# A mixture-of-experts kernel: gate and up units of whole rows, runs of 8192 bytes, activation work in the down stage

## What is computed

```python
D_MODEL, SEQ, N_EXPERTS, TOP_K, D_EXPERT = 1024, 512, 32, 4, 1024

def clamped_swiglu_expert(xb, w_gu, b_gu, w_dn, b_dn):
    gu = xb @ w_gu + b_gu
    x_glu, x_lin = gu[..., :D_EXPERT], gu[..., D_EXPERT:]
    x_glu = jnp.minimum(x_glu, SWIGLU_LIMIT)
    x_lin = jnp.clip(x_lin, -SWIGLU_LIMIT, SWIGLU_LIMIT)
    act = x_glu * jax.nn.sigmoid(SWIGLU_ALPHA * x_glu) * (x_lin + 1.0)
    return act @ w_dn + b_dn
```

## Time and profile before

| | us |
|---|---|
| median of 3 runs | 1479.59 (1477.33 to 1483.07) |
| profiled execution | 1484.01 |
| its span | 1482.2 |
| first matmul of the loop's first round | 347.02 |
| first down matmul of the last expert | 1452.19 |

### The profile page before, as it was taken

How to read it: one execution, slowest core, us unless ns; L and a number is a source line. 1 busy time by engine, 2 the same in 40 slices (tenths; PEclk the granted TensorE clock), 3 DMA queues, 4 the chain that set the end, 5 groups by cost and what they waited for, 6 DMA issues and landing times.

```text
span 1482.2 us, 19488 instructions
## 1 busy us (share of the span) xinstructions
PE 1397.9 (94%) x6520; PEld 1151.0 (78%) x6520; DVE 1233.7 (83%) x927; ACT 1025.6 (69%) x750; POOL 451.3 (30%) x231
## 2 busy tenths in 40 slices
PE   6999998967999999999999999999999999999995
PEld 5877886855888888788778877877888888788774
DVE  5534545367999999999999999999999999999997
ACT  5234332365888887877778778878877887877774
POOL 0000000275233533333333334433333333333301
PEclk9999998978999999999999999999999999999998
DMA  8311324366999999999999999999999999999994
GB/s 304 102 58 57 100 71 132 117 203 230 369 388 385 387 374 369 369 371 371 362 365 367 359 357 375 366 362 370 365 365 379 372 368 372 371 369 363 369 358 147
DMA packets 129145, 453.48 MB, mean 306 GB/s; under 512 B 13887, under 2 KB 13903, under 8 KB 128992
## 3 DMA queue, kind: packets, MB, share of 16 engines
q1 hardware_dynamic: 117096, 432.55, 78.4%
q0 software_dynamic: 10304, 18.26, 4.8%
q10 hardware_dynamic: 1720, 2.34, 0.5%
HBM read 447.63 MB, written 22.59 MB: 317 GB/s over the span
## 4 chain that ended last, share of the span: by engine, by line
PE 70%; DMA 12%; DVE 6%; issue 6%; ACT 4%; POOL 2%; SPq 0%; ACTq 0%; DVEq 0%; POOLq 0%
PE ps L1670 17%; PE ps L1678 16%; PE ps L1672 16%; DMA raw<-in_w_down 4%; PE ps L1401 4%; PE ps L1402 4%; PE ps L1407 4%; DVE wlo L974 4%; DMA raw_b<-in_w_gate_up 4%; ACT whi L682 3%; DMA raw<-in_w_gate_up 2%; PE ps L1648 1%; PE ps L1661 1%; POOL slot_table L600 1%; DMA xg<-h_rows,idx_gather 1%
## 5 line engine op out<-in xcount | busy, mean ns | idle before, releaser
L974 DVE TENSOR_TENSOR wlo<-raw,whi 128x2048 fp32r<-128x2048 f32 x274 | 646.0, 2394 | 126.3 <-ACT whi L682 125.4
L682 ACT ACTIVATE whi<-raw 128x2048 fp32r<-128x2048 f32 x274 | 521.9, 1915 | 207.3 <-DMA raw<-in_w_down 97.0
L1670 PE MATMUL ps<-whi,xT_hi 128*128 128x512 f32 x1040 | 412.7, 397 | 36.0 <-issue 22.1
L1672 PE MATMUL ps<-whi,xT_lo 128*128 128x512 f32 x1040 | 406.8, 391 | 0.0
L1678 PE MATMUL ps<-wlo,xT_hi 128*128 128x512 f32 x1040 | 279.2, 390 | 0.2 <-DVE wlo L974 0.2
L1670 PEld LDWEIGHTS ps<-whi,xT_hi 128*128 128x128 f32 x1040 | 196.3, 189 | 86.9 <-issue 42.9
L1678 PEld LDWEIGHTS ps<-wlo,xT_hi 128*128 128x128 f32 x1040 | 195.6, 188 | 41.9 <-DVE wlo L974 0.9
L1672 PEld LDWEIGHTS ps<-whi,xT_lo 128*128 128x128 f32 x1040 | 196.5, 189 | 39.1
L1670 PE MATMUL ps<-whi,actT_hi 128*128 128x512 f32 x496 | 196.0, 395 | 0.0
L1672 PE MATMUL ps<-whi,actT_lo 128*128 128x512 f32 x496 | 193.3, 390 | 0.0
L682 ACT ACTIVATE whi<-raw_b 128x2048 fp32r<-128x2048 f32 x64 | 122.6, 1916 | 50.6 <-DMA raw_b<-in_w_gate_up 44.6
(11 more groups left out here) (217 smaller groups left out, 1591.0 us busy)
## 6 DMA issues: line engine op xcount, KB each, us to landing
raw<-in_w_gate_up SPq DMA_DIRECT2D x130, 1024.0 KB, 12.0
raw<-in_w_down SPq DMA_DIRECT2D x126, 1024.0 KB, 13.1
raw_a<-in_w_gate_up SPq DMA_DIRECT2D x63, 1024.0 KB
raw_b<-in_w_gate_up SPq DMA_DIRECT2D x63, 1024.0 KB
raw<-in_w_in SPq DMA_DIRECT2D x14, 1024.0 KB, 5.2
raw<-in_w_out SPq DMA_DIRECT2D x4, 1024.0 KB, 5.1
x<-in_x SPq DMA_DIRECT2D x4, 512.0 KB, 8.1
acc_rows<-x SPq DMA_DIRECT2D x4, 512.0 KB, 4.8
```

Source lines behind the costliest of these rows:

```text
L682: nc.scalar.activation(whi_slot(n), raw_slot(slot_of(n)), ACT.Copy).then_inc(hi_done, 1)
L974: nc.vector.tensor_tensor(wlo_slot(n), raw_slot(slot_of(n)), whi_slot(n).bitcast(F32), ALU.subtract).then_inc(lo_done, 1)
L1670: mm(ps[:, bank + half, :], x_hi_t[:, k0 + k, :], w_hi_ap, start=k0 + k == 0 and not started, stop=False, skip_group_check=started)
L1672: mm(ps[:, bank + half, :], x_lo_t[:, k0 + k, :], w_hi_ap, start=False, stop=False, skip_group_check=started)
```

## The change

- A gate/up unit is now 128 whole rows of 2048 columns, one run of 8192 bytes on each partition. Its four parts of 512 columns go to the four banks 0 to 3. All eight units add to all four banks, so that gate and up sums are both complete only behind unit 7. Expert 0 keeps the old units (`first_gate_up`).
- `w_down` lies on partitions by `(p k)`: partition p holds rows 8p to 8p + 7, and a unit is two of them, one run of 8192 bytes at a pitch of 32 KB. The columns of the activations are read to match: `features` transposes every eighth column of `act`, where it took 128 neighbours.
- `sigmoid` waits for all eight gate/up units. On ACT and DVE the activation work stands together behind them, and `tokens_hi`, `tokens_lo` and the two bias copies behind or among it.
- The wait for the up bias stands ahead of the third part of unit 0.
- The branch for full experts follows suit.

```diff
-    wdn_v = w_down[0].rearrange("e (k p) c -> p e k c", p=P)
+    wgu_rows = w_gate_up[0].rearrange("e (k p) c -> p e k c", p=P)
+    wdn_v = w_down[0].rearrange("e (p k) c -> p e (k c)", p=P)
...
+            def gate_up_rows(e, u):
+                return wgu_rows[:, e, u, :].rearrange("p e c -> p (e c)")
+
             def down_source(e, u):
-                return wdn_v[:, e, KM * u:KM * u + KM, :]
+                return wdn_v[:, e, UNIT * u:UNIT * u + UNIT]
...
-                act_e.wait_ge(used, i * U_E + (U_MOE + U_GU // 2 if e == 0 else U_LOOP + (e - 1) * U_E + U_GU // 2))
+                act_e.wait_ge(used, i * U_E + (U_MOE + U_GU // 2 if e == 0 else U_LOOP + (e - 1) * U_E + U_GU))
...
-                    last = nc.tensor.transpose(ps[:, 6 + j // 4, (j % 4) * P:(j % 4 + 1) * P], act[:, j * P:(j + 1) * P], ident)
+                    last = nc.tensor.transpose(ps[:, 6 + j // 4, (j % 4) * P:(j % 4 + 1) * P], act[:, :].rearrange("p (f k) -> p k f", k=KD)[:, j, :], ident)
...
+            def gate_up(n0, e, i=0):
 
                 pe.wait_ge(x_hi, i + (e + 1))
                 pe.wait_ge(x_lo, i + (e + 1))
                 pe.wait_ge(bias_gate, i + (e + 1))
                 for u in range(U_GU):
-                    if u == 2 and e > 0:
+                    if u == 2:
                         features(e - 1, i)
...
+                    hi_ready(n0 + u, i)
+                    for part in range(4):
+                        if u == 0 and part == 2:
+                            pe.wait_ge(bias_lin, i + (e + 1))
+                        w_hi_ap, _ = unit_part(n0 + u, part)
+                        mm(ps[:, part, :], xT_hi[:, u, :], w_hi_ap, start=False, stop=False, skip_group_check=True)
+                        mm(ps[:, part, :], xT_lo[:, u, :], w_hi_ap, start=False, stop=False, skip_group_check=True)
+                    lo_ready(n0 + u, i)
+                    for part in range(4):
+                        _, w_lo_ap = unit_part(n0 + u, part)
+                        last = mm(ps[:, part, :], xT_hi[:, u, :], w_lo_ap, start=False, stop=u == U_GU - 1,
+                                  skip_group_check=True)
+                    last.then_inc(used, 1)
```

More of the change, by code:

```diff
@@ L416, in _, with load @@
         def _(sp):
-            def load(n, i, source):
+            def load(n, i, source, rows):
                 if last_in_slot(n) is not None:
@@ L898, in _ @@
             hi(33, i)
-            sigmoid(1, i)
             act_e.wait_ge(x_tr, E)
@@ L903, in _ @@
                 act_e.dma_start(bdn_raw[r:r + E, :], b_down[0]).then_inc(bdn_in, 16)
-            for n in (34, 35, 36, 37, 38):
+            for n in (34, 35, 36):
+                hi(n, i)
+            sigmoid(1, i)
+            for n in (37, 38):
                 hi(n, i)
@@ L1738, in _, with over_gate_up, over_down @@
                     with pe.If(i < total):
[L1739 to L1740 removed]
+                        def over_gate_up():
+                            for u in range(U_GU):
+                                pe.wait_ge(v_full[u % RAW], i * (16 * U_E // RAW) + 16 * (u // RAW + 1))
+                                for part in range(4):
+                                    last = mm(ps[:, part, :], xT32[:, u, :], raw[:, u % RAW, part * UW:(part + 1) * UW],
+                                              start=False, stop=(u == U_GU - 1))
+                                last.then_inc(v_free, 1)
+                        def over_down():
+                            for u in range(U_GU, U_E):
                                 pe.wait_ge(v_full[u % RAW], i * (16 * U_E // RAW) + 16 * (u // RAW + 1))
                                 for k in range(KM):
[L1743 removed]
+                                    kk = KM * (u - U_GU) + k
                                     for half in range(2):
                                         col = k * MW + half * UW
[L1746 to L1747 removed]
+                                        last = mm(ps[:, 4 + half, :], actT32[:, kk, :], raw[:, u % RAW, col:col + UW],
+                                                  start=(kk == 0), stop=(kk == KD - 1))
                                 last.then_inc(v_free, 1)
@@ L1767, in _ @@
                                start=True, stop=False)
-                        for q in range(2):
-                            whole_matrix(q, xT32, True)
+                        over_gate_up()
                         pe.wait_ge(v_act, i + 2)
                         for j in range(KD):
-                            last = nc.tensor.transpose(ps[:, 6 + j // 4, (j % 4) * P:(j % 4 + 1) * P], act[:, j * P:(j + 1) * P], ident)
+                            last = nc.tensor.transpose(ps[:, 6 + j // 4, (j % 4) * P:(j % 4 + 1) * P], act[:, :].rearrange("p (f k) -> p k f", k=KD)[:, j, :], ident)
                         last.then_inc(v_tr, 1)
                         pe.wait_ge(v_aT, i + 1)
-                        whole_matrix(2, actT32, False)
+                        over_down()
                         pe.wait_ge(v_y, i + 1)
```

87 lines of the change are left out of this document (38 added, 49 removed).

## The result

| | us |
|---|---|
| kernel before, median of 4 | 1479.88 |
| changed kernel, median of 4 | 1457.47 (1456.08 to 1457.89) |
| ratio | 0.9846, 95% interval 0.9826 to 0.9866 |
| profiled execution, its span | 1457.89, 1456.1 |

The change is worth 1.5%, more than twice the 0.65% of the forecast.

What follows compares the result with a forecast made beforehand. Loads were taken to pace the loop from about 595 us. Profiled 1484.01 - 12.7 (long runs) + 1.4 (stride) + 1.0 (last round) = 1473.7 us, as a median 1469.3, stated as 1470; range 1448 to 1495.

Steps and rivals of the forecast that it cites:

- What bounds the loop, the floor, and what PE would need: Expert loop from about 595 us: loads set 35.70 us a round; PE's floor is 34.46, needing 378 GB/s.
- The wait for `tokens_lo`: PE's wait at round start: follows from late loads; removed there, its 1.24 us return at the next lo part.
- Runs of 8192 bytes, +1.5%: Weight loads in the loop: half as many packets raise the DMA rate 1.5%, saving 0.53 us a round, -12.7 us.
- the line through 2 KB and 4 KB: Upper bound for long load packets: 20.5 ns per packet is not bytes; halving the packets saves 6%.
- the 8 KB row on ACT's queue: Lower bound for long load packets, from the mix constants' transfer: 44.0 us of an engine per MB, 2% worse.
- losses in bursts: Loop loads: rate lost in bursts not caused by many packets, 298 GB/s while POOL issues the scatter, 410 before.
- Order, layout of gate and up, w_down by `(p k)`: each 0: Loop: gate/up matmul order, activation work moved behind those units, and w_down's 32 KB pitch each change nothing.
- Stride, +1.4: Strided transposes of `act`: +0.2 us a round, showing only in the seven rounds before 595 us, +1.4 us.
- Last round, +1.0: Last round of the loop: the last features wait for `act`, +1 us.
- The hole on DVE: Four activation steps in a row, 4.9 us without splitting: loads do not run dry; a rival had PE starved, median 1490.
- at +3.6% the floor is reached: Rival for the loop: 8 KB runs give 378 GB/s, DMA falls behind PE, -25 us, median 1456; chance 0.15.

Runs made afterwards that it cites:

- e7: Kernel before without the indirect scatter of y in the loop (a 64-byte write instead, sums over experts not computed): 1454.24 us, ratio 0.9821.
- e8: Kernel before with one DVE step moved, `tokens_lo` ahead of the `lo` of unit 38: 1487.45 us, ratio 1.0030.
- e2: Changed kernel, same addresses and order, each run of 8192 bytes cut into two packets of 4096: 1460.78 us, ratio 0.9873.
- e4: Kernel before with only the changed kernel's order of steps on ACT and DVE: 1473.78 us, ratio 0.9947.
- e3: Kernel before with only w_down by `(p k)` in runs of 8 KB and strided transposes: 1470.26 us, ratio 0.9930.
- e13: Changed kernel with w_down in blocks and contiguous transposes as before, whole gate/up rows cut into two 4 KB packets: 1463.79 us, ratio 0.9876.
- e10: Kernel before with the changed kernel's order of steps on DVE alone: 1492.06 us, ratio 1.0057.

## Why the prediction was wrong, by its own steps

- *What bounds the loop, the floor, and what PE would need.* Right. The loads paced (the waits of ACT say so; the DMA share of 1.00 alone would not, see e7), the floor is 34.46 us, and it is reached at 380 GB/s where 378 was worked out. The wait for `tokens_lo` was a symptom (e8).
- *Runs of 8192 bytes, +1.5%, the whole of the gain.* The first failed step: mis-sized, and wrongly taken for all there was. The longer packets take 3.1% off the price (e2 against the changed kernel), and bring only 0.27 of the 1.54%, as the floor cuts off the rest. Both ends of my bound came from poor rows: the line through 2 KB and 4 KB gave 20.5 ns a packet from a mixer stretch that was 70% busy, and the 8 KB row on ACT's queue had 709 packets for 1.08 MB, so most of them were not 8 KB at all. I weighed towards that row "of the right kind". The middle, 3 to 4%, was the better choice and lies at the 3.6% that the floor needs; whether the long packets would reach the floor by themselves no run shows.
- *The reason for staying low: losses in bursts that belong to the scatter and not to packets.* Half right. Without the scatter the gap is closed (e7), and by the records it takes 1.3 us of all engines in a round. But cheaper loads close the gap just as well, so this was no reason to take a small gain.
- *Order, layout of gate and up, w_down by `(p k)`: each 0.* Wrong, the second failed step, and in time the larger one: with these three and packets of 4 KB, e2 is 1.27% faster, twice the whole forecast. I had counted packets only. In the kernel before, the order is worth 0.5% (e4), w_down in 8 KB runs 0.7% (e3), and whole rows in 4 KB packets take e4 from 0.995 to 0.988 (e13). These gains overlap, since PE's floor caps them all. In the sum, 21 rounds at 34.47 instead of 35.70 are -25.8 us of the measured 1484.01 - 1457.89 = 26.1, where I had -12.7.
- *Stride, +1.4.* Against 0.01 us a round, nothing. *Last round, +1.0.* Right in place and about in size: PE waits 2.13 us for `act` and 0.53 for `y`, against 2.02 for `y` before; 30.0 us from there to the end became 31.2.
- *The hole on DVE.* It costs PE only where loads are late (e4, e10), at the place named. That the loads do not run dry in it was wrong for e4, where one load in a round comes up to 3.9 us late. In the changed kernel no PE wait for `wlo` is left in the loop, as the loads run ahead of it.
- *Rivals and chances.* The forecast's own sentence had it: at +3.6% the floor is reached. The price fell by 7%, of which the floor lets PE use about half. That the direction was right is in part luck: most of the gain came by edits that had been put at nothing. With three edits that all touch the loads and a cap only 3.6% away, 0.15 was too little for it.

## What to carry to other kernels

Work out how far the next bound is before you estimate the size of a gain: here it was 3.6% away, and each of the things that touched the loads went some way to it, so the end was far easier to name than the terms. In these kernels a packet cost its bytes and, with all else the same, about 10 ns, and a bound for that is only as good as the purity of the packets in the row that it comes from. The indirect add into HBM took twice the engine time per byte of a load by the records, and where loads pace it is the first thing to count. An order of steps that adds no work can still change what a load takes (e4: 41.5 us of an engine per MB for 42.7), so an edit that moves no bytes is not to be put at nothing unseen. Once the loop sits at its floor, look at the waits at its two ends: moving the 8.3 us at the start brought 7.0 there, 5.1 of them for good.

## What the runs showed of the hardware that I had not expected

- The indirect scatter with addition took 88 us of one DMA engine per MB (difference of before and e7) against 43 for the gather and for loads in 4 KB packets.
- The 16 DMA engines were recorded as busy all of the time in e7, where no load was waited for. A full share is no proof of a bound.
- After 8.3 us without a matmul the granted clock of PE was 0.50, and the next unit took 5.28 us instead of 2.72.
- The order of steps on ACT and DVE changed the engine time of a load from 42.7 to 41.5 us per MB with the same packets and addresses, and by 0.4 only where the scatter is left out. Five slots instead of six gave 42.4, and 0.4 us a round. The cause is open.
- With gate and up in whole rows of 8 KB, one block of 1 MiB, the price was 41.1 against 41.5 with 256 half rows, at equal packets of 4 KB; one trace of each.
- A strided stationary operand lengthens the record of a weight load from 140 to 188 ns, and eight transposes in a row were no slower (0.01 us a round).
- The DMA moved 380 GB/s over 741 us with 3% of its engines' time unused. The Trainium skill (DMA: Bandwidth & Descriptors, Where 436 GB/s comes from) puts the limit for HBM at about 358 GB/s for each core, half of what a stack gives its two; with one core at work this kernel goes past it.
